# Second block of a two-block kernel: value products one step later, in-chunk products inside the recurrence, exponents on VectorE

## The reference

```
h = rms_norm(x); cols = h @ w_in
y_gdn  = gated delta rule, 6 heads of 64, both directions, chunks of 64 tokens
y_mla  = softmax attention, 6 heads: q, k of 96 columns, v of 64
y_rwkv = RWKV-7 recurrence (decay mixer), 4 heads of 64, both directions
x = x + (concat(y_gdn, y_mla, y_rwkv) * silu(gate)) @ w_out
```

```
diff = cum[i] - cum[j];  d_incl = exp(where(i >= j, diff, -inf))
a_mat = beta * (k k^T) * strict(d_incl);  p_intra = (q k^T) * d_incl
gam = exp(cum);  q_g = q * gam
u0, w = solve(I + a_mat, [beta v, beta gam k])
u = u0 - w S;  o = q_g S + p_intra u;  S = exp(cum_end) S + k_d^T u
```

## Time and profile before

| | |
|---|---|
| median of 3 runs | 2225.78 us (2225.41 to 2228.92) |
| the profiled execution | 2220.6 us, span 2218.4 us |
| TensorE, its clock | busy 1866.7 us (84%), mean 0.947 of full |
| VectorE | busy 777.7 us (35%) |
| ScalarE | busy 591.2 us (27%) |
| GpSimd | busy 223.8 us (10%) |
| chain that ended last | TensorE 71%, VectorE 11%, ScalarE 5% |
| first block, first layer, second layer | 919 us, 644 us, 647 us of the span |

### The profile page before, as it was taken

How to read it: one execution, slowest core, us unless ns; L and a number is a source line. 1 busy time by engine, 2 the same in 40 slices (tenths; PEclk the granted TensorE clock), 3 DMA queues, 4 the chain that set the end, 5 groups by cost and what they waited for, 6 DMA issues and landing times.

```text
span 2218.4 us, 45669 instructions
## 1 busy us (share of the span) xinstructions
PE 1866.7 (84%) x18488; PEld 1069.3 (48%) x18488; DVE 777.7 (35%) x1445; ACT 591.2 (27%) x994; POOL 223.8 (10%) x273
## 2 busy tenths in 40 slices
PE   5999983877777775799998889979899997899887
PEld 2444532444444442357765853344358756743443
DVE  1233424111111111536556731350455557522431
ACT  3014521000000000334315423250243244232331
POOL 0002213111111110001003000001001012000001
PEclk9999996999999998899999999999999999899999
DMA  9563022999999996220000012100110000031101
GB/s 354 203 240 121 7 81 71 389 421 422 420 413 417 420 425 258 94 69 31 3 2 2 4 66 67 62 1 29 66 67 4 3 2 2 3 118 38 39 1 38
DMA packets 72048, 303.54 MB, mean 137 GB/s; under 512 B 8860, under 2 KB 20364, under 8 KB 54848
## 3 DMA queue, kind: packets, MB, share of 16 engines
q1 hardware_dynamic: 62240, 287.49, 32.8%
q0 software_dynamic: 5872, 9.68, 1.3%
q10 hardware_dynamic: 3760, 3.85, 0.5%
HBM read 296.67 MB, written 12.71 MB: 139 GB/s over the span
## 4 chain that ended last, share of the span: by engine, by line
PE 71%; DVE 11%; another core or an unknown queue 7%; ACT 5%; issue 3%; DMA 1%; ACTq 1%; DVEq 0%; POOLq 0%; SPq 0%; POOL 0%
PE bank L2070 11%; PE bank L458 11%; PE bank L2086 5%; PE bank L935 5%; PE bank L487 5%; PE bank L480 4%; PE bank L1912 3%; PE bank L2008 2%; PE bank L906 2%; DVE arena L1423 1%; ACT arena L947 1%; PE bank L1947 1%; PE bank L920 1%; PE bank L1934 1%
## 5 line engine op out<-in xcount | busy, mean ns | idle before, releaser
L2070 PE MATMUL bank<-arena 128*64 128x256 f32 x2048 | 241.4, 391 | 85.8 <-remote 85.8
L458 PE MATMUL bank<-hT,arena 128*128 128x512 f32 (+1 forms) x640 | 294.7, 617 | 13.1 <-DVE hT L2630 7.7
L2070 PEld LDWEIGHTS bank<-arena 128*64 128x64 f32 x2048 | 150.6, 140 | 189.0 <-issue 130.0
L480 PE MATMUL bank<-arena 64*64 64x64 f32 x6656 | 213.9, 220 | 22.6 <-DVE arena L1546 7.4
L480 PEld LDWEIGHTS bank<-arena 64*64 64x64 f32 x6656 | 202.6, 135 | 36.6 <-DVE arena L1546 10.5
L458 PEld LDWEIGHTS bank<-hT,arena 128*128 128x128 f32 (+1 forms) x640 | 124.7, 197 | 177.9 <-issue 160.4
L2578 DVE COPY arena<-bank 128x256 f32<-128x256 f32 x32 | 13.6, 425 | 377.5 <-PE bank L2078 377.5
L2086 PE MATMUL bank<-arena 128*64 128x512 f32 x512 | 118.6, 605 | 17.3 <-remote 17.3
L947 ACT ACTIVATE arena<-bank 128x512 f32<-128x512 f32 (+3 forms) x146 | 86.2, 591 | 157.3 <-PE bank L458 92.3
L487 PE MATMUL bank<-hT,arena 128*128 128x512 f32 x224 | 108.5, 622 | 16.5 <-ACTq L948 16.5
L935 PE MATMUL bank<-arena 128*128 128x512 f32 x256 | 110.4, 593 | 0.0
(11 more groups left out here) (413 smaller groups left out, 2562.9 us busy)
## 6 DMA issues: line engine op xcount, KB each, us to landing
arena<-w_gate SPq DMA_DIRECT2D x32, 2048.0 KB, 15.3
arena<-w_up SPq DMA_DIRECT2D x32, 2048.0 KB
arena<-w_down SPq DMA_DIRECT2D x32, 2048.0 KB, 11.3
arena<-w_ada SPq DMA_DIRECT2D x12, 2048.0 KB, 19.4
arena<-w_in SPq DMA_DIRECT2D x10, 2048.0 KB, 12.0
arena<-w_out SPq DMA_DIRECT2D x6, 2048.0 KB, 8.0
arena<-w_in SPq DMA_DIRECT2D x6, 1536.0 KB, 6.8
arena<-y_scratch SPq DMA_DIRECT2D x4, 1024.0 KB, 7.9
```

What stands on the lines that cost most here:

```text
L458: m = pe.matmul(bank[b][lo:lo + w, :], slot2(n)[:, k, c:c + w], hT[:, k, :], start=(k == 0), stop=(k == KD - 1))
L480: m = pe.matmul(o[half(f), s, t], lhs[half(f), s, t], rhs[half(f), s, t], start=True, stop=True)
L2070: mm = pe.matmul(bank[b][c * CAP:(c + 1) * CAP, 0:FE // 2], XT[j][:, k % 4, k // 4, :], slot(ring_at + i)[:, k, c * (FE // 2):(c + 1) * (F ...
```

## The change

Three places of the second block, in each layer.

1. GDN's decay exponents. TensorE keeps only the running sum (`decay_rows`). VectorE adds the key term out of PSUM into `g_V` and takes the minimum with the mask (`exponents`), and ScalarE takes the exponent of `g_V` in place. For head pair 0 both `decay_rows` and `token_rows` are issued ahead of the ninth column, in banks 2 and 3, and VectorE's part ahead of the ninth convolution. VectorE's first chain goes one direction after the other up to its transpose; the products of L1406 come after both, and ScalarE's first copy over `g_V` waits for them. The exponent `gam` goes to `g_WT`, and the queries are scaled after doubling levels 2 and 3.
2. RWKV's in-chunk products. They accumulate in banks 6 and 7 during the recurrence, 16 a step, over a zero written by four products of 512 columns with a zero block of `blk`. The state increments move into banks 4 and 5. The outputs stage loses its in-chunk products; lengths and means use banks 4 and 5.
3. Attention. The value products come at even i for p = (i - 6) / 2, between scores and transposes. The scale goes into ScalarE's copy of the queries; the maximum is negated by the reduction itself and signals ScalarE without a second operation. Gating moves to iterations 13 and 21 and signals by a semaphore of its own.

Some semaphores also take other names (`first_only`, `y_slots`).

```diff
+            def decay_rows(ht, b):
+                for d in range(2):
+                    c = 6 * d + 2 * ht
+                    name = "F" if d == 0 else "B"
+                    for s in range(2):
+                        for t, f in pairs_in:
+                            m = pe.matmul(pieces(bank[b + d])[half(f), s, t], g_g[half(f), t, c + s:c + s + 1].to_broadcast([CG, CG]),
+                                          const2("cum" + name)[half(f), half(f)], start=True, stop=True)
+                    m.then_inc(sem(f"g_e_args{d}"), 1)
+            def token_rows(ht):
+                for d in range(2):
+                    c = 6 * d + 2 * ht
+                    for t in range(TT):
+                        for s in range(2):
+                            m = pe.matmul(bank[4 + d][half(s), ts(t)], g_g[:, t, c + s:c + s + 1].to_broadcast([P, CG]),
+                                          const2("cumF" if d == 0 else "cumB"), start=True, stop=True)
+                    m.then_inc(sem(f"g_gam_args{d}"), 1)
...
-                    for d in range(2):
-                        c = 6 * d + 2 * ht
-                        name = "F" if d == 0 else "B"
-                        for f in range(2):
-                            i64 = ident[half(f), half(f)]
-                            o = bank[d][half(f), :]
-                            pe.matmul(blocks(o), i64, over_blocks(const2("far" + name)[half(f)], CG), start=True, stop=False)
-                            start_of = g_c2[half(f), :, c:c + 2].rearrange("p t (s o) -> p s t o", o=1)
-                            pe.matmul(pieces(o), i64, start_of.to_broadcast([CG, 2, TT, CG]), start=False, stop=False)
...
-                    if ht > 0:
+                    if ht == 0:
+                        for b in (0, 1):
+                            pe.wait_ge(bank_free[b], 1)
+                    else:
+                        decay_rows(ht, 0)
                         for d in range(2):
                             uw_free[d].wait()
+                        token_rows(ht)
...
             def rwkv_recurrence():
                 state, u_full = [[Count(pe, sem(f"{n}{d}")) for d in range(2)] for n in ("g_s_full", "g_u_full")]
+                def z(i, s, t, f):
+                    return bank[6 + f][half(s), i * 256 + t * CG:i * 256 + (t + 1) * CG]
+                def values_within(lo, hi):
+                    for j in range(lo, hi):
+                        i, t, d, s, f = j // 32, j // 8 % 4, j // 4 % 2, j // 2 % 2, j % 2
+                        h = 2 * i + s
+                        pe.matmul(z(i, s, t, f), r_vtok[half(f), t, h * GD:(h + 1) * GD], pieces(r_PkT[:, i, d])[half(f), s, t],
+                                  start=False, stop=False)
+                def updates_within(n):
+                    for i in range(2):
+                        for s in range(2):
+                            for d in range(2):
+                                t, f = divmod(chunk_at(d, n), 2)
+                                m = pe.matmul(z(i, s, t, f), r_u0[d][half(f), t, 2 * i + s, :], pieces(r_PbT[:, i, d])[half(f), s, t],
+                                              start=False, stop=(n == NC_G - 1 and i == 1))
+                    return m
+                def keys_values(d, t, f, i):
+                    for s in range(2):
+                        pe.matmul(bank[4 + d][half(s), i * GD:(i + 1) * GD], r_kmtok[half(f), d, t, 2 * i + s, :],
+                                  r_vtok[half(f), t, (2 * i + s) * GD:(2 * i + s + 1) * GD], start=True, stop=False)
+                for f in range(2):
+                    for s in range(2):
+                        pe.matmul(bank[6 + f][half(s), :], blk[half(f), half(1 - f)], over_blocks(const2("I64")[half(f)], CG),
+                                  start=True, stop=False)
                 for n in range(NC_G):
                     if n > 0:
                         for d in range(2):
...
                     if n < NC_G - 1:
                         for d in range(2):
                             t, f = divmod(chunk_at(d, n), 2)
-                            for i in range(2):
-                                for s in range(2):
-                                    pe.matmul(bank[4 + 2 * d + i][half(s), 0:GD], r_kmtok[half(f), d, t, 2 * i + s, :],
-                                              r_vtok[half(f), t, (2 * i + s) * GD:(2 * i + s + 1) * GD], start=True, stop=False)
+                            keys_values(d, t, f, 0)
+                    if n > 0:
+                        values_within(8 * n, 8 * n + 4)
                     for d in range(2):
                         t, f = divmod(chunk_at(d, n), 2)
                         if n > 0:
                             u_full[d].wait()
                         if n < NC_G - 1:
                             for i in range(2):
+                                if i == 1:
+                                    keys_values(d, t, f, 1)
                                 for s in range(2):
-                                    m = pe.matmul(bank[4 + 2 * d + i][half(s), 0:GD], r_btok[half(f), d, t, 2 * i + s, :],
+                                    m = pe.matmul(bank[4 + d][half(s), i * GD:(i + 1) * GD], r_btok[half(f), d, t, 2 * i + s, :],
                                                   r_u0[d][half(f), t, 2 * i + s, :], start=False, stop=True)
                             m.then_inc(sem(f"g_inc_done{d}"), 1)
+                    values_within(8 * n + 4 if n > 0 else 0, 8 * n + 8)
+                    m = updates_within(n)
+                m.then_inc(sem("g_z_done"), 1)
...
                     m.then_inc(sem("g_x_done"), 1)
-                    for t in range(TT):
-                        for s in range(2):
-                            h = 2 * i + s
-                            for d in range(2):
...
-                    m.then_inc(sem("g_z_done"), 1)
...
+                    if i == 8:
+                        for d in range(2):
+                            take(pe, bank_free[2 + d])
+                        decay_rows(0, 2)
+                        for d in range(2):
+                            pe.wait_ge(bank_free[4 + d], 1)
+                        token_rows(0)
...
                 n = MH * TT
-                for i in range(n + 4):
+                for i in range(n + 5):
                     if i < n:
                         h, q = 2 * (i // 8) + i % 2, (i % 8) // 2
                         take(pe, bank_free[i % 4])
                         pe.matmul(bank[i % 4][:, :], m_q[0:QK_M, h, ts(q)], m_k[0:QK_M, h, :], start=True,
                                   stop=True).then_inc(for_dve[i % 4], 1)
-                    if 3 <= i < n + 3:
-                        j = i - 3
-                        pe.wait_ge(sem("probs_ready"), j + 1)
-                        to_tokens(4 + j % 2, m_pr[:, j % 4, :])
-                    if i >= 5 and i % 2 == 1:
-                        p = (i - 5) // 2
+                    if i >= 6 and i % 2 == 0:
+                        p = (i - 6) // 2
                         hp, q = p // TT, p % TT
                         pe.wait_ge(sem("turned_ready"), 2 * p + 2)
...
+                    if 3 <= i < n + 3:
+                        j = i - 3
+                        pe.wait_ge(sem("probs_ready"), j + 1)
+                        to_tokens(4 + j % 2, m_pr[:, j % 4, :])
...
                 for ht in range(3):
                     for d in range(2):
-                        e_args[d].wait()
-                        act.activation(g_V[d], bank[d], ACT.Exp).then_inc(sem(f"g_e_full{d}"), 1)
+                        e_in[d].wait()
+                        act.activation(g_V[d], g_V[d], ACT.Exp).then_inc(sem(f"g_e_full{d}"), 1)
...
+                            if l == 1:
+                                pt_full[d].wait()
...
-                    move(b, m_q[0:QK_M, h, :], bank[b][0:QK_M, :])
+                    move(b, m_q[0:QK_M, h, :], bank[b][0:QK_M, :], scale=QK_M ** -0.5)
...
                         chain(act.activation(m_pr[:, i % 4, :], bank[i % 4][:, :], ACT.Exp, bias=m_st[:, i % 4, 0:1],
-                                             scale=QK_M ** -0.5, accum_out=m_st[:, i % 4, 1:2]))
+                                             accum_out=m_st[:, i % 4, 1:2]))
...
-                            act.wait_ge(sem("turned_used"), j // 2 - 1)
+                            p = j // 2 - 2
+                            if p % TT == TT - 1:
+                                act.wait_ge(sem("heads_gated"), p // TT + 1)
+                            else:
+                                act.wait_ge(sem("turned_used"), p + 1 - p // TT)
...
+                def exponents(ht, b):
+                    for d in range(2):
+                        c = 6 * d + 2 * ht
+                        key_term = g_c2[:, :, c:c + 2].rearrange("p t (s o) -> p s t o", o=1).to_broadcast([P, 2, TT, CG])
+                        e_args[d].wait()
```

(45 more changed lines are left out.)

80 lines of the change are left out of this document (32 added, 48 removed).

## The result

Over four runs each, the changed kernel takes 2160.45 us (2157.02 to 2163.92) against 2225.6 us (2222.72 to 2228.92): ratio 0.9713, 95% interval [0.9686, 0.9739]. The profiled execution took 2157.02 us with a span of 2154.7 us; before, it was 2220.6 and 2218.4. So 63.6 us of profiled time are gone, where 51 were forecast.

What follows compares the result with a forecast made beforehand. TensorE, busy 84%, was taken to bound the kernel, with a ring of waits binding attention. Attention 30, GDN 15 and RWKV 6 sum to 51 us: profiled 2220.6 to 2169.6, 2175 on the median; range 2158 to 2198.

Steps and rivals of the forecast that it cites:

- The ring: Attention: a 5.13 us repeat of waits through TensorE, VectorE and ScalarE; later value products open it, repeat 3.9 us.
- A: Rival, attention: the ring is loosened, not opened; repeat stays near 4.7 us, 38 us gained in all, 2188; chance 0.15.
- C: Rival, attention: runs at 1.2 GHz throughout, 7.1 us a repeat, slower than before at 2252 us; chance 0.03.
- The lower end: Attention: low bound of the 30 us gain, 10 us, if only L1660's 0.3 us comes off the ring and tail.
- A wait less at the start: Attention's early tiles: one wait less, with 0.3 us less for each early tile, gives 1.5 us a layer.
- its ends: GDN, head pair 0: bounds of -1 and +3 us around the 1 us gain taken.
- D: Rival: VectorE's exponents and the convolution set each head pair's start; GDN gives nothing; 20 us in all, 2205; chance 0.05.
- The sum for the first layer: RWKV, first layer: 6.8 freed in outputs, less 1.5 zero products, 1.0 steps, 0.5 behind the last: 3.8 us.
- between: RWKV, second layer: 2 us taken between -3.6 (clock stays at 1.2 GHz) and 7.1 (added work brings it back).
- the gap: RWKV outputs, first layer: 1.3 us within the in-chunk products' 4.05 us; the second layer was counted without it, at 5.8.
- B: Rival, RWKV: added products drop TensorE to 1.2 GHz in both recurrences, -10 instead of +6, 2191; chance 0.14.

## Why the prediction was right, and where it was off

**Attention (30 forecast, 30.7 measured).** The ring was the cause and the value products' place opened it: A, a loosened ring, falls with the repeat of 3.78 us, and so does C, with clocks of 0.94. The eight repeats of the steady stretch take 31.1 us in both layers, the gated ones included, for 31.2 in the forecast. The forecast repeat of 3.9 took ScalarE's 1.96 us a tile, in which 0.25 was the wait for VectorE; with the signal moved up it is 1.89. The lower end, "10 us, if only the 0.3 us of L1660 comes off", is what the separate operation measured in the closed ring, 10.3. "A wait less at the start" did not come: the gating of two heads stood in it, as the later gating shows.

**GDN (15 forecast, 18.1 in the stages).** TensorE's queue, again in the second layer, for the earlier trace rows:

```profile
1659.59 2.03 PE L500 MATMUL bank<-arena 64*64 64x64 f32 x61
1661.55 1.97 PE L509 MATMUL bank<-arena 128*64 128x128 f32 x32
...
1663.94 7.03 PE L489 MATMUL bank<-hT,arena 128*128 128x512 f32 x16
1670.90 2.08 PE L482 MATMUL bank<-arena 64*64 64x64 f32 x64
```

Decay rows to token rows are 1.96 us against 5.41, a gain of 3.45 for the 3.5 forecast, and the first doubling product starts behind the column without a wait. From pair products to pair products, head pairs 1 and 2 give 3.6 and 3.7 us in the second layer, 3.8 and 3.7 in the first: 7.3 and 7.5 where 6.5 was counted. Head pair 0, forecast at 1, gives 3.7 and 4.7 us in the chunks for the 4.1 moved into the columns, -0.4 and +0.6, within its ends. By these the part is worth 6.9 + 8.1 = 15.0, the forecast, of which 1.0 is the clock: three other kernels with the same chunks take 36.15 us for the first layer's head pair 0, where the changed kernel took 35.17, with a clock of 0.95 against 0.91 over the pair. The other 3.1 us is the second layer's columns, where 4.1 us were added and 1.0 shows, because less of them ran at 1.2 GHz (clock 0.94 on average, 0.90 before). Of the seven kernels with these columns four take 85.4 or 85.5 us there and three 87.6, 88.5 and 88.9. So three of the 63.6 us can't be put down to the change. D falls with the whole.

**RWKV (6 forecast, 15.1 measured): the step that was mis-sized.** The sum for the first layer said 3.8, and 5.8 came; for the second, 2 taken "between" -3.6 and 7.1, and 9.3 came. The outputs stage is shorter by 7.4 us in each (14.6 to 7.1, from its first lengths to the first mean) where 6.8 and 5.8 were counted. The in-chunk products themselves held TensorE for what was counted, 6.8 us in the first layer and 2.7 + 3.1 in the second, where the gap did not recur:

```profile
1942.97 3.78 PE L473 MATMUL bank<-sq,c_sb 128*128 128x512 f32 x4 [1.31 <-remote]
...
1949.06 0.27 PE L771 MATMUL bank<-arena 64*64 64x64 f32 x1
...
1951.80 1.12 PE L473 MATMUL bank<-sq,c_sb 128*128 128x512 f32 x2
...
1954.42 0.27 PE L771 MATMUL bank<-arena 64*64 64x64 f32 x1
...
1957.55 1.12 PE L847 MATMUL bank<-arena,c_sb 128*128 128x512 f32 x2
```

The other 0.6 and 1.6 us stand in the lengths and state products. Behind thin steps these began at 0.50 in both layers of the kernel before, the first four instructions taking 3.65 and 3.78 us, against 1.98 in the changed kernel; waits for ScalarE's squares took part of that back. The sum had no such term. The recurrence with the zero products takes 18.0 us in both, where it took 16.3 and 19.9. In the first layer that is 1.7 more, not 3.0. The zero products delay the first step by 0.92 us for 1.5:

```profile
1885.27 1.10 PE L748 MATMUL bank<-arena,c_sb 64*64 64x512 f32 x8 [2.57 <-ACT arena L1188]
1886.19 0.30 PE L744 MATMUL bank<-arena 64*64 64x64 f32 x8
...
1891.74 0.91 PE L757 MATMUL bank<-arena 64*64 64x64 f32 x14
...
1896.28 0.92 PE L757 MATMUL bank<-arena 64*64 64x64 f32 x14
```

Two steps are 4.54 us, 2.27 each against 2.15, so the added 0.68 us costs 0.12, near the 0.15 forecast. In the second layer the clock decided: the recurrence got 1.9 us shorter, where the middle of the two outcomes has it 3.8 longer, and these 5.7 us are most of the miss. I had both outcomes and took the middle, which no kernel shows: the fuller steps ran at 1.00 from the second step on in every kernel that had them. That the total stayed within the range is owed to the width of the range, and not to this term. B was thus the wrong way round: it is the thin steps that fall, and the products that were thought to cost something at 1.2 GHz are what prevents it. The two rows could not show that. They hold the same 336 instructions, thin steps both, and say only that thin steps are found at either clock; in the kernels with the wait filled and with the products behind, the first layer fell in the steps as well. The trace of before had no fuller step to compare with.
